# Two-block transformer, fused on one core: the attention of the differential heads is done beside tiles 13 to 22 of the in-projection, and the decay is computed at tile 3

## The reference

```python
proj = h @ w_in                       # 1024 -> 3 x 1024 + 6
qa, ka, va, qb, kb, vb, qc, kc, vc, fz = jnp.split(proj, cuts, axis=-1)
# A, 4 heads: two softmax maps of width 32, rope; a = p[:, :, 0] - lam * p[:, :, 1]; a @ va; rmsnorm of the output
# B, 6 heads of width 64: rope, dilated mixture of windows
# C, 6 heads of width 64: scores + cumsum(log_sigmoid(fz + bias)) of the query less that of the key
o = concat(oa, ob, oc) @ w_out
x = x + gate1 * o
# then the MLP: w_up, causal conv of width 3, silu(g) * u, w_down
```

## Time and profile before

| | |
|---|---|
| median of 3 runs | 2477.89 us (2474.12 to 2480.39) |
| profiled execution, its own time | 2476.35 us |
| its span | 2474.5 us |
| granted TensorE clock, mean | 0.956 |
| busy: TensorE, VectorE, ScalarE | 92%, 49%, 35% of the span |
| instructions | 31,727 |

### The profile page before, as it was taken

How to read it: one execution, slowest core, us unless ns; L and a number is a source line. 1 busy time by engine, 2 the same in 40 slices (tenths; PEclk the granted TensorE clock), 3 DMA queues, 4 the chain that set the end, 5 groups by cost and what they waited for, 6 DMA issues and landing times.

```text
span 2474.5 us, 31727 instructions
## 1 busy us (share of the span) xinstructions
PE 2271.0 (92%) x11320; PEld 1566.1 (63%) x11320; DVE 1207.4 (49%) x2319; ACT 855.3 (35%) x1564; POOL 80.8 (3%) x84
## 2 busy tenths in 40 slices
PE   6999999999998999889999999989987799888886
PEld 3776567888886684678888867758855333333332
DVE  6555756525526547765435445766343322323235
ACT  4224734323323226633223345464342121212123
POOL 0000000000000000000000000000000211111110
PEclk8997999999999996999999999999998899999998
DMA  7761054223333740043233312203315699999996
GB/s 270 236 187 52 2 191 115 88 91 103 102 78 103 229 128 18 5 116 102 77 102 102 113 58 85 94 14 126 125 45 236 237 385 389 418 402 400 407 395 266
DMA packets 214548, 414.31 MB, mean 167 GB/s; under 512 B 20951, under 2 KB 177249, under 8 KB 197857
## 3 DMA queue, kind: packets, MB, share of 16 engines
q1 hardware_dynamic: 200833, 398.68, 45.2%
q0 software_dynamic: 11520, 8.43, 1.1%
q10 hardware_dynamic: 2016, 4.81, 0.5%
HBM read 420.24 MB, written 25.17 MB: 180 GB/s over the span
## 4 chain that ended last, share of the span: by engine, by line
PE 75%; DMA 9%; DVE 7%; issue 4%; ACT 3%; SPq 1%; ACTq 0%; DVEq 0%; PEldq 0%; PEld 0%; POOLq 0%
PE bank L736 10%; PE bank L738 10%; PE bank L737 10%; DMA arena<-in_expert_up_w 8%; PE bank L664 7%; PE bank L665 6%; PE bank L666 6%; PE bank L1106 5%; PE bank L1107 3%; PE bank L783 2%; PE bank L1115 2%; PE bank L757 2%; PE bank L773 2%; PE bank L613 2%; PE bank L691 1%
## 5 line engine op out<-in xcount | busy, mean ns | idle before, releaser
L1106 PE MATMUL bank<-arena,xT 128*64 128x512 f32 x560 | 265.8, 632 | 49.7 <-DMA arena<-in_expert_up_w 37.7
L664 PE MATMUL bank<-hT_r,arena_r 128*128 128x512 f32 x704 | 287.9, 409 | 22.5 <-DVE arena_r L1652 10.3
L666 PE MATMUL bank<-hT_r,arena_r 128*128 128x512 f32 x704 | 277.4, 394 | 0.0
L738 PE MATMUL bank<-hT_r,arena_r 128*128 128x512 f32 x704 | 275.0, 391 | 0.0
L1107 PE MATMUL bank<-arena,xT 128*64 128x512 f32 x560 | 266.2, 633 | 0.0
L665 PE MATMUL bank<-arena_r 128*128 128x512 f32 x656 | 258.9, 395 | 0.0
L2239 DVE TENSOR_TENSOR hT<-hT,bank 64x512 f32<-64x512 f32 x80 | 54.8, 685 | 322.7 <-PE bank L1094 294.5
L737 PE MATMUL bank<-arena_r,S_r 128*128 128x512 f32 x528 | 206.8, 392 | 0.0
L1106 PEld LDWEIGHTS bank<-arena,xT 128*64 128x64 f32 x560 | 79.2, 145 | 166.9 <-issue 151.3
L664 PEld LDWEIGHTS bank<-hT_r,arena_r 128*128 128x128 f32 x704 | 134.2, 191 | 78.4 <-issue 13.1
L666 PEld LDWEIGHTS bank<-hT_r,arena_r 128*128 128x128 f32 x704 | 134.3, 191 | 29.4
(11 more groups left out here) (434 smaller groups left out, 4374.9 us busy)
## 6 DMA issues: line engine op xcount, KB each, us to landing
arena<-in_expert_gate_w SPq DMA_DIRECT2D x32, 2048.0 KB, 14.6
arena<-in_expert_up_w SPq DMA_DIRECT2D x32, 2048.0 KB, 19.4
arena<-in_expert_down_w SPq DMA_DIRECT2D x32, 2048.0 KB, 20.0
arena<-in_w_up SPq DMA_DIRECT2D x88, 512.0 KB, 5.1
arena<-in_w_in SPq DMA_DIRECT2D x68, 512.0 KB, 6.1
arena<-in_w_mod SPq DMA_DIRECT2D x32, 1024.0 KB, 7.7
arena<-in_w_down SPq DMA_DIRECT2D x40, 512.0 KB, 3.9
S<-in_w_mod SPq DMA_DIRECT2D x16, 1024.0 KB, 5.0
```

The source lines that it names most:

```text
L664: mm(b[:, :], w_h, hT_r[:, k, :], start=start, stop=False)
L666: return mm(b[:, :], w_l, hT_r[:, k, :], start=False, stop=stop)
L738: return mm(b[:, :], w_slot(arena_r, i, piece)[:, at:at + P], hi, start=False, stop=stop)
L1106: mm(bank[half][gate0:gate0 + SUB, :], x, expert_weights(slot, 0)[:, k, :], start=k == 0, stop=k == KD - 1)
```

## The change

The 16 jobs of A are taken out of the attention and done in 19 slots, `n = 0` to `18`: two in each of tiles 13 to 21 (one in the middle of the tile's matmuls, one at its end) and one in the middle of tile 22. In slot `n` TensorE multiplies with v for the jobs `n - 4` and `n - 3` (n even), transposes job `n - 2` and makes the scores of job `n`; ScalarE copies the transposed job `n - 2` and exponentiates job `n`; VectorE takes the maximum of job `n` and normalises job `n - 1`. Scores are in banks 2 and 3, transposes in bank 4, outputs in bank 6 (first pair) and 5 (second pair); probabilities are in `tmp` alone. The outputs are copied before the rest of the attention, which goes through `LATER`, the 24 jobs of B and C, by the old routine without its branches for A. The fold of the modulation goes into the bank that gathered it and is added to the columns in two steps. `FZ_AT` becomes 3: TensorE's matmuls for fz stand behind tile 3, and VectorE's whole chain stands in its stream at tile 5, ahead of the rope of tile 6.

```diff
-FZ_AT = 13
+FZ_AT = 3
+EARLY_AT = 13
+EARLY = sum(1 for job in JOBS if job[0] == "A")
+LATER = JOBS[EARLY:]
+EARLY_SLOTS = EARLY + 3
...
+        def early_slots(h, half):
+            n = 2 * (h - EARLY_AT) + half
+            return [n] if 0 <= n < EARLY_SLOTS else []
...
             def proj_half(b, i, j, lo, between=None):
                 for k in range(KD):
                     ins = proj_mm(b, i, k, j, lo(k), k == 0, k == KD - 1)
+                    if k == KD // 2 - 1 and between is not None:
+                        between()
...
+            def early(l, n):                                   # TensorE
+                if n >= 4 and n % 2 == 0:
+                    done = n - 4
+                    _, _, g, qb = JOBS[done]
+                    pe.wait_ge(s["pt_ready"], l * PTILES + (done + 2))
+                    for kb in range(qb + 1):
+                        for m in range(2):
+                            ins = mm(early_bank(g // 2)[HD * m:HD * m + HD, qb * P:(qb + 1) * P], v[:, kb, (g + m) * HD:(g + m + 1) * HD],
+                                     turned(m)[:, kb * P:(kb + 1) * P], start=kb == 0, stop=kb == qb)
+                    ins.then_inc(s["pv_done"], 2)
+                if 2 <= n < EARLY + 2:
+                    job = n - 2
+                    pe.wait_ge(s["p_ready"], l * PTILES + (job + 1))
+                    if job:
+                        pe.wait_ge(s["pt_ready"], l * PTILES + job)
+                    for kb in range(JOBS[job][3] + 1):
+                        ins = nc.tensor.transpose(bank[4][:, kb * P:(kb + 1) * P], early_probs(2 * job + 1)[:, kb * P:(kb + 1) * P], ident)
+                    ins.then_inc(s["t_done"], 1)
+                if n < EARLY:
+                    if n:
+                        pe.wait_ge(s["max_ready"], l * UNITS + 2 * n)
+                    else:
+                        pe.wait_ge(s["rope_done"], l * len(ROPE) + TURNED)
+                    layer_scores(JOBS[n], (bank[2], bank[3]))
...
+            def early(l, n):                                   # VectorE
+                if n < EARLY:
+                    w = (JOBS[n][3] + 1) * P
+                    for m in range(2):
+                        u = 2 * n + m
+                        dve.wait_ge(s["s_done"], l * UNITS + (u + 1))
+                        if n >= 2:
+                            dve.wait_ge(s["t_done"], l * PTILES + (n - 1))
+                        ...
+                if 1 <= n <= EARLY:
+                    job = n - 1
+                    dve.wait_ge(s["exp_done"], l * UNITS + (u1 + 1))
+                    ...
...
                 for h in range(2 * IN_SLOTS):                  # VectorE
                     if h in ROPE:
                         ...
+                    for n in (*early_slots(h, 0), *early_slots(h, 1)):
+                        early(l, n)
+                    if h == FZ_AT + 2:
+                        decay(l)
+                    elif h % 2 and h < 2 * IN_SLOTS - 1:
                         proj_rest(l, (h + 1) // 2 + 1)
+                    if h in FOLD_AT:
+                        m = FOLD_AT.index(h)
+                        add_columns(l * MOD_BLOCKS + (m + 2), (GT1, SC2)[m], bank[5 + 2 * m])
...
-                attention(JOBS, l * UNITS, l * PTILES, l * len(JOBS), lambda p: (hT if p < 2 else hT_r)[:, p, :])
+                for pair in range(2):                          # ScalarE
+                    act.wait_ge(s["pv_done"], l * len(JOBS) + EARLY // 2 * (pair + 1))
+                    af(hT[:, pair, :], early_bank(pair)[:, :], ACT.Copy).then_inc(s["o_copied"], 1)
+                attention(LATER, l * UNITS + 2 * EARLY, l * PTILES + EARLY, l * len(JOBS) + EARLY, lambda p: hT_r[:, p, :])
```

More of the change, by code:

```diff
@@ L301, in last_of_pair @@
         def last_of_pair(job):
-            return job[3] == NT - 1 and (job[0] != "A" or job[2] % 2 == 1)
+            return job[3] == NT - 1
         def sub_tmp(t):
@@ L314, in probs, with early_probs, early_bank @@
             return S[:, u % NS, :] if u % (2 * NS) < NS else tmp[:, (u % NS) * T:(u % NS + 1) * T]
+        def early_probs(u):
+            return tmp[:, (u % 4) * T:(u % 4 + 1) * T]
+        def early_slots(h, half):
+            n = 2 * (h - EARLY_AT) + half
+            return [n] if 0 <= n < EARLY_SLOTS else []
+        def early_bank(pair):
+            return bank[6 if pair == 0 else 5]
         def place(i):
@@ L614, in mod_products, with mod_fold @@
                 ins.then_inc(s["mod_used"], 1)
-            def mod_fold(done, sums, block):
+            def mod_fold(done, sums, b):
                 pe.wait_ge(s["mod_copied"], done)
-                at = 2 * KD * block
                 for j in range(4):
-                    ins = mm(bank[6][:, at + j:at + 2 * KD - 3 + j:4], sums[:, j * P:(j + 1) * P], ident[:, 0:P - 31:32], start=True, stop=True)
+                    ins = mm(b[:, j:2 * KD - 3 + j:4], sums[:, j * P:(j + 1) * P], ident[:, 0:P - 31:32], start=True, stop=True)
                 ins.then_inc(s["mod_turned"], 1)
@@ L681, in proj_pair, with proj_token @@
                             ins.then_inc(s["tiles_done"], 1)
-            def proj_token(b, i, j, lo):
+            def proj_token(b, i, j, lo, between=None):
                 for t in range(2):
+                    if t and between is not None:
+                        between()
                     cols = slice((2 * j + t) * P, (2 * j + t + 1) * P)
@@ L738, in split_mm, with attention @@
                 return mm(b[:, :], w_slot(arena_r, i, piece)[:, at:at + P], hi, start=False, stop=stop)
-            def attention(jobs, U, N, J, Q, scores, lows=None):
+            def attention(jobs, U, N, J, Q, scores, lows=None, copied=None):
                 n = len(jobs)
@@ L750, in attention @@
                         jj = j - LAG
+                        if jj == 0 and copied is not None:
+                            pe.wait_ge(s["o_copied"], copied)
                         for tile in range(tile0[jj], tile0[jj + 1]):
-                            u = 2 * jj + (1 if jobs[jj][0] == "A" else tile - tile0[jj])
+                            u = 2 * jj + tile - tile0[jj]
                             pe.wait_ge(s["p_ready"], N + (tile + 1))
@@ L818, in _ @@
                             half = proj_half if h in QK_OF else proj_token
[L819 removed]
+                            half(bank[h % 2], i, j, normed_lo, lambda: [early(l, n) for n in early_slots(h, 0)]).then_inc(s["tiles_done"], 1)
                         if MOD_AT <= h < MOD_AT + MOD_REST:
@@ L1827, in attention @@
                         r0, r1 = mx[:, 0, c:c + 1], mx[:, 0, c + 1:c + 2]
[L1828 to L1834, removed]
+                        for u, r in ((u0, r0), (u1, r1)):
+                            vec.tensor_scalar(probs(u)[:, 0:w], probs(u)[:, 0:w], r, None, ALU.mult).then_inc(s["p_ready"], 1)
                     if after is not None:
@@ L1843, in out_rest @@
             def out_rest(l, j):
-                done = [job[2] // 2 for i, job in enumerate(JOBS) if last_of_pair(job) and (i + LAG + 4 == j or j == len(JOBS) and i + LAG + 4 > j)]
+                done = [job[2] // 2 for i, job in enumerate(LATER) if last_of_pair(job) and (i + LAG + 4 == j or j == len(LATER) and i + LAG + 4 > j)]
                 for pair in done:
-                    if pair >= 2:
-                        out_low(pair, l * PAIRS + (pair + 1), h_lo[:, pair, :], bank[6 + pair % 2][:, :])
+                    out_low(pair, l * PAIRS + (pair + 1), h_lo[:, pair, :], bank[6 + pair % 2][:, :])
             proj_rest(0, 0)
```

82 lines of the change are left out of this document (54 added, 28 removed).

## The result

The changed kernel takes 2460.11 us (median of four, 2459.75 to 2464.04) where the kernel before has 2477.66 beside it (2474.12 to 2480.39): ratio 0.9934, interval 0.9921 to 0.9947. That is 17.6 us less; the forecast was 2455, 23 us less. The profiled execution is the longest of the four (2464.04, span 2462.2). A second profile of the same kernel, taken with the experiments (median 2458.63, ratio 0.9928, 0.9915 to 0.9942), has a span of 2456.8. I read both, because they differ in where the clock falls.

What follows compares the result with a forecast made beforehand. TensorE was taken as the bound, at half clock in the first kind's attention. Per layer −39.9 + 22.4 + 2.5 + 0.7 + 2.5 + 0.3 = −11.5, two layers −23.0, giving 2455 us; own range 2448 to 2462, widened to 2444 to 2468.

Steps and rivals of the forecast that it cites:

- What stays of the attention: Attention after the projection: 24 jobs of the other two kinds, started cold, take 63.4 us a layer; 0.3 charged for copies.
- The first kind's TensorE work at full clock: In the projection: scores, transposes and products with v of the 16 K = 32 jobs add 22.4 us a layer.
- visits: In the projection: TensorE going to the small jobs and back costs 0.19 us each, 13 charged, 2.5 us a layer.
- Waits in tiles 13 to 22: In these projection tiles: TensorE waits twice, behind tile 19 and in tile 21, 0.7 us a layer.
- The decay's move: Decay moved to tile 3 of the projection: VectorE's chain delays its later work, TensorE waits 2.5 us before tile 10.
- The forecast's sign of being right: In the in-projection: it is 28 us longer, with granted clock 1.00 in every stretch.
- Past the attention nothing changes: Everything behind the attention: no change in time, so no term in the sum.
- A rule against the change: In the projection: the skill's rule that transposes do not count as busy speaks against mixing them in; the clock could fall.
- TensorE sets the time on both sides: In the old projection and the first kind's attention: TensorE is the bound, the other two engines have room beside the projection.

## Why the forecast held, and where it was off

The sign and the mechanism held, and the time lies inside the forecast's own range. At the second block, behind all that was changed, the gain is 14.7 and 14.5 us in the two profiles and not 23.0: 3.7 are missing in the two layers of the first and 4.6 behind them. That the medians come out at 17.6 and 18.2 is in part luck, from the last 830 us, for which the forecast has nothing. By its steps:

**What stays of the attention (63.4 + 0.3).** 64.4 and 64.5 us, 63.0 and 64.3 in the second profile. The short fall of the clock was in the sum, taken over from the second block's start. Right within 1 us.

**The first kind's TensorE work at full clock (22.4) and visits (2.5).** Together with the waits 26.4 by leaving the jobs out, where these terms have 25.6. The visits were priced right: 2.4, with those that share a tile's end with the modulation free. The lengths read from K = 64 scores held for K = 32 ones (0.91 for 384 columns is 0.85 and the lap of 0.07; 11.8 in all, 11.9 forecast), and the products have their 5.6. The transposes were priced too low, 6.3 where 5.0 was forecast: I had read eight in a row, and one to four at a time, ahead of scores, take 0.26, 0.37, 0.48 and 0.59, which is 0.11 each and 0.15 for every job.

**Waits in tiles 13 to 22 (0.7).** 0.3 in sum, with the spacing of the slots as the reason: without it they are 19.1.

**The decay's move (2.5).** The wait was there, in the place, from the releaser and within 0.12 us of the length forecast. The clock that it can take with it (1.7 us in one of two layers) was not in the sum. It shows in the whole projection: in the first profile it is 30.9 us longer in layer 0 and 28.0 in layer 1, each from its first matmul, where 28.1 was forecast. 26.4 + 2.4 = 28.8, and 1.7 more where the clock falls; the rest is the half clock at a layer's start, which costs 0.6 more than before in layer 0 and 1.0 less in layer 1. The forecast's sign of being right, 1.00 in every stretch of the projection, missed by this fall. And the wait was avoidable: the cut and earlier chain is 8.5 us faster.

**"Past the attention nothing changes."** This is the step that failed. The instructions there are the same, and so is the first wait; the clock isn't. The wait for toep behind the attention is 2.02 us in both kernels. The stretch around it, in the kernel before (behind 316.36):

```profile
316.00:326.00 10.00, 7.98 (x38) 5.78 (x35) 7.59 (x6) 5.78 (x7) 0.00 (x0) 1.00 0.80 306
```

and in the changed kernel behind 308.13:

```profile
308.00:318.00 10.00, 7.98 (x28) 5.47 (x25) 7.82 (x6) 5.78 (x7) 0.00 (x0) 0.83 0.82 317
```

The same 7.98 us busy at 1.00 and at 0.83, which is less work done in the second. I summed (1 − granted clock) × 5 us over rows of 5 us like these. From the end of layer 1's attention to the second block the kernel before loses 8.5 us and the changed one 13.6 in both profiles; between layer 0's attention and layer 1 it is 3.4 and 5.1. Together 6.8 us more, and of the 19.3 us of the two layers 4.6 are gone at the second block (19.3 − 14.7). This is the larger part of the 8.3 us missing there. What decides at such a stop whether the clock falls stays open: with the same work and the same wait some 8 us earlier it came out otherwise, and no run here separates the moment from what was done before it.

**A rule against the change.** The granted clock is 1.00 in all of 140 to 240, with transposes and K = 32 scores mixed in. The Trainium skill ("TensorE: Matmul & The Clock Gate", Part 4) says that transposes do not count as busy for the clock; no run here puts transposes alone to the test, and as a reason against mixing them into dense work it did not bear. Part 1 of that page says that a busy engine is given the full clock; A's old stretch stays at 0.50 when wholly busy, but one full-array matmul a job holds it at 1.00 in layer 0, even where TensorE is then less busy (4.15 of 5 us). Part 1 also says that the length of the cold start differs between runs of one kernel. The two profiles of the changed kernel agree for the start of layer 0's projection, where the clock costs 3.0 us in one and 2.7 in the other. That the wait at tile 10 brings half clock in one and not in the other (2.38 and 2.37 us) is another matter, a fall and not a start, and is left open.

**What the change is worth, and why.** In the forecast 37.6 us at half clock become 22.4 at full clock. That reads as if the clock were the gain. For the most part it is not: with the clock at 1.00 in the old place the jobs still take 32 to 34 us, as VectorE does not get through them faster; that is 4 to 6 us of the 37.6. The gain is that VectorE's and ScalarE's part now lies beside matmuls that TensorE has to do anyway, so that only TensorE's own work and the visits count, 26.4 us. My sentence that TensorE sets the time on both sides was right for the old kernel at its old clock and would have misled anyone who repaired the clock alone.

## What to carry to other kernels

A stage in which one engine is wholly busy at half clock can be bound by another engine right behind it; before repairing the clock, add up what the others need at full clock (here 32 to 34 us against 37.6), and look instead for a neighbouring stage with room for their part. When small jobs are laid into a dense stage, the distance between them decides: the same work half a tile apart cost 26.4 us a layer, and two at a time 34 us more. An idle time moved or added should be priced with the clock it may take along, and before a long chain is moved on an in-order engine, look what urgent work will stand behind it: here cutting it and beginning it earlier took the wait away.

## What the runs showed of the hardware

- Wholly busy is not enough: 33.5 of 33.5 us busy with K = 32 scores, transposes and products of 64 rows stays at 0.50, and one full-array matmul of 512 columns a job beside the same work keeps it at 1.00 in both layers. With 256 columns it held in layer 0 and not in layer 1.
- Stops of 2.0 to 2.7 us cost the clock in some places and executions and not in others (2.66 us at the attention's start: a fall in layer 0, none in layer 1 of one profile). It also fell behind 1.02 and 0.85 us, one after the other, and once behind 1.25 us.
- Breaking a projection tile's accumulation in its middle for fp32 matmuls into another bank and going on costs little: 0.09 us on the way in and 0.10 on the way out, in the middle of a tile as at its end.
